# Split-product attention scores for the later query blocks, later selection rounds, and layer statistics with tokens on partitions

## What is computed

```
h = layer_norm(alpha * h + 0.5 * swiglu(h, ffn1...))          # first norm
h = layer_norm(alpha * h + hybrid_mixer(h, ...))              # second norm
h = layer_norm(alpha * h + 0.5 * swiglu(h, ffn2...))
...
# layer_norm
mu = mean(x); var = mean(square(x - mu)); (x - mu) * rsqrt(var + eps) * g + b
...
# attention, for each query block: top-k of the index scores, then
s = einsum('bqhc,bqkc->bqhk', q_lat, kv_sel) * ATT_HEAD_DIM ** -0.5
p = softmax(where(valid, s, -inf))
o = einsum('bqhk,bqkc->bqhc', p, kv_sel)
```

## Time and profile before

| what | us |
|---|---|
| median of 3 runs (lowest, highest) | 1013.48 (1012.99, 1014.37) |
| the profiled execution | 1013.6 |
| its span | 1011.9 |
| first FFN and first norm, until the first projection starts | 0 to 373.5 |
| projections, scan, selection | 373.5 to 530.3 |
| attention loop | 530.3 to 596.6 |
| output projection and second norm | 596.6 to 652.5 |
| second FFN and last norm | 652.5 to 1011.9 |

### The profile page before, as it was taken

One profiled execution on the slowest core, in us unless ns is written; L12 is line 12 of the kernel. 1 busy time (PEld: TensorE's weight loads), 2 busy tenths in 40 slices (PEclk: granted clock), 3 DMA queues, 4 the chain that ended last, 5 costly groups with the idle time before them and its releaser, 6 DMA issues.

```text
span 1011.9 us, 19045 instructions
## 1 busy us (share of the span) xinstructions
PE 992.6 (98%) x7048; PEld 911.2 (90%) x7048; DVE 718.1 (71%) x1299; ACT 500.2 (49%) x883; POOL 120.5 (12%) x96
## 2 busy tenths in 40 slices
PE   8999999999999999999999999999999999999996
PEld 8999999999999989699866778889999999988885
DVE  6988888888223263599998633699989989932336
ACT  6655655566221254546336732566656665812121
POOL 0000000000211253044221205310000000000000
PEclk9999999999999999999999999999999999999998
DMA  7223232323222323131210102113323233333212
GB/s 253 85 88 121 87 120 83 124 70 115 87 86 87 106 75 107 43 123 50 80 42 1 43 1 84 42 42 126 124 83 124 93 114 105 126 96 106 93 57 84
DMA packets 30847, 90.47 MB, mean 89 GB/s; under 512 B 4688, under 2 KB 5328, under 8 KB 30800
## 3 DMA queue, kind: packets, MB, share of 16 engines
q1 hardware_dynamic: 30800, 89.83, 27.0%
HBM read 87.72 MB, written 2.10 MB: 89 GB/s over the span
## 4 chain that ended last, share of the span: by engine, by line
PE 80%; DVE 15%; ACT 2%; issue 1%; DMA 1%; SPq 0%; DVEq 0%; ACTq 0%
PE ps L1253 38%; PE ps L1311 22%; PE ps L1176 9%; DVE sc L2244 3%; DVE top L2243 3%; PE ps L1448 1%; PE ps L1716 1%; PE ps L1730 1%; DVE qk L2283 1%; PE ps L1756 1%; DVE wlo L1920 1%; PE ps L1513 1%; PE ps L1361 1%; PE ps L1359 1%; DMA wraw<-in_ffn_w_up 1%
## 5 line engine op out<-in xcount | busy, mean ns | idle before, releaser
L1253 PE MATMUL ps<-tsum,whi 128*128 128x264 f32 (+1 forms) x1280 | 243.1, 282 | 0.5 <-ACT ht L813 0.5
L1253 PEld LDWEIGHTS ps<-tsum,whi 128*128 128x128 f32 x1280 | 202.3, 188 | 0.7 <-issue 0.7
L1253 PE MATMUL ps<-tsum,wlo 128*128 128x264 f32 (+1 forms) x640 | 180.3, 282 | 0.0
L1253 PE MATMUL ps<-xh,whi 128*128 128x264 f32 (+1 forms) x480 | 135.4, 282 | 0.3 <-ACT sil L813 0.3
L1253 PE MATMUL ps<-xl,whi 128*128 128x264 f32 (+1 forms) x480 | 135.5, 282 | 0.0
L752 ACT ACTIVATE whi<-wraw 128x1408 fp32r<-128x1408 f32 (+1 forms) x48 | 74.7, 1556 | 122.9 <-PE ps L1311 121.8
L1253 PE MATMUL ps<-xh,wlo 128*128 128x264 f32 (+1 forms) x480 | 135.3, 282 | 0.0
L1830 DVE TENSOR_TENSOR wlo<-wraw,whi 128x1408 fp32r<-128x1408 f32 (+1 forms) x38 | 70.1, 1845 | 85.9 <-ACT whi L752 85.9
L1311 PE MATMUL ps<-hh,whi 128*128 128x264 f32 (+1 forms) x462 | 124.2, 323 | 0.0
L1311 PE MATMUL ps<-hh,wlo 128*128 128x264 f32 (+1 forms) x462 | 123.5, 322 | 0.0
L1311 PE MATMUL ps<-hl,whi 128*128 128x264 f32 (+1 forms) x462 | 123.3, 321 | 0.0
(11 more groups left out here) (304 smaller groups left out, 1854.2 us busy)
## 6 DMA issues: line engine op xcount, KB each, us to landing
wraw<-in_ffn_w_gate SPq DMA_DIRECT2D x43, 512.0 KB, 4.2
wraw<-in_ffn_w_up SPq DMA_DIRECT2D x42, 512.0 KB, 4.4
wraw<-in_ffn_w_down SPq DMA_DIRECT2D x32, 384.0 KB, 3.2
wraw<-in_ffn_w_down SPq DMA_DIRECT2D x32, 320.0 KB, 3.5
wraw<-in_w_in SPq DMA_DIRECT2D x19, 512.0 KB, 4.4
wraw<-in_w_out SPq DMA_DIRECT2D x8, 512.0 KB, 4.4
out<-zrow SPq DMA_DIRECT2D x8, 256.0 KB, 2.0
x<-in_x SPq DMA_DIRECT2D x3, 528.0 KB, 7.5
```

The costliest lines, as they stand in the source:

```text
L1253: mm = pe.matmul(ps[:, bank, 0:(HT, HALF_SEQ)[p // 2]], w[:, k * P:(k + 1) * P], v[:, k, :], start=(first and k == 0 and n == 0), stop=(k ...
```

## The change

It has three parts, in one diff.

1. **Split-product scores.** For j of 3 and 4 (k of 16 and up) a score product is three f32r products: high part of the queries by high part of the keys, low part of the queries by high part of the keys, high part of the queries by low part of the keys. POOL makes all parts: `split_keys_hi` before `split_latents`, and behind it `split_queries` (two casts and two subtractions, each 128x4x256, waiting for the third head of `normed_mlstm`) and `split_keys_lo` (a subtraction, 128x528). PE waits for the six of them (`att_split`) at k=16. The high parts of the queries lie in `xh` and `xl`, which are free then.
2. **Selection rounds.** `LATE_AT` becomes (3, 4, 5).
3. **Layer statistics with tokens on partitions.** The sum tiles are now the stationary operand and one column of `mean_w` moves. p=0: 12 fp32 products of 88 token columns by one column for each half; p=1: 8 of 128. The statistics are then [88, 3] or [128, 2] wide on ACT and DVE. `spread_stat` brings mean and inverse deviation back to all partitions: 3 (p=0) or 2 (p=1) fp32 products with the identity, 88 or 128 columns wide, for each of both halves and both values. For p=0, e=0 they stand inside the down product, after kk=10 and kk=17. DVE's first scales of a half wait for the spread.

```diff
-LATE_AT = (2, 3, 4)
+LATE_AT = (3, 4, 5)
...
+SPLIT_J = 3
...
+    ql_low = sb("ql_low", [P, ATT_H, T], F32R, s)
...
+def query_hi(h):
+    return (xh if h < 4 else xl)[:, h % 4, :]
...
+def stat_tiles(p, e):
+    R = (HT // 3, P)[p]
+    t0 = e * HT if p == 0 else N_META + e * HALF_SEQ
+    return [(i, R, slice(t0 + i * R, t0 + (i + 1) * R)) for i in range(3 - p)]
+def token_sums(p, e, v):
+    return ps[0:(HT // 3, P)[p], 4 + 2 * v + e, 320:320 + 3 - p]
+def token_stat(p, e, v):
+    return stat[0:(HT // 3, P)[p], e, 4 * v:4 * v + 3 - p]
...
+        def split_keys_hi():
+            pool.wait_ge(ct_ready, 1)
+            pool.tensor_copy(ct_hi[:, :], ct[:, :]).then_inc(att_split, 1)
+        def split_keys_lo():
+            pool.wait_ge(att_split, 1)
+            pool.wait_ge(ql_done, ATT_H)
+            pool.tensor_tensor(ct_lo[:, :], ct[:, :], ct_hi[:, :].bitcast(F32), ALU.subtract).then_inc(att_split, 1)
+        def split_queries():
+            pool.wait_ge(ql_own, QL_DVE)
+            pool.wait_ge(ql_ready, ATT_H - QL_DVE)
+            pool.wait_ge(hn_ready, 3)
+            for e, v in enumerate((xh, xl)):
+                pool.tensor_copy(v[:, 0:4, LATE_T], ql[:, 4 * e:4 * e + 4, LATE_T]).then_inc(att_split, 1)
+            for e, v in enumerate((xh, xl)):
+                q = ql[:, 4 * e:4 * e + 4, LATE_T]
+                pool.wait_ge(att_split, e + 2)
+                pool.tensor_tensor(ql_low[:, 4 * e:4 * e + 4, LATE_T], q, v[:, 0:4, LATE_T].bitcast(F32), ALU.subtract).then_inc(att_split, 1)
         mix_lo(N_PROJ)
+        split_keys_hi()
         split_latents()
+        split_queries()
+        split_keys_lo()
...
-            act.activation(part(sil[:, 0, :], p, e), part_bank(4, p, e), ACT.Square).then_inc(s["mu2_done"], 1)
+            act.activation(token_stat(p, e, 0), token_sums(p, e, 0), ACT.Copy).then_inc(s["mu2_done"], 1)
+            act.activation(token_stat(p, e, 1), token_sums(p, e, 0), ACT.Square).then_inc(s["mu2_done"], 1)
             act.wait_ge(s["varc_done"], e + 1)
-            act.activation(part(sil[:, 1, :], p, e), part_bank(6, p, e), ACT.Sqrt).then_inc(s["sd_done"], 1)
+            act.activation(token_stat(p, e, 3), token_stat(p, e, 2), ACT.Sqrt).then_inc(s["sd_done"], 1)
...
                 if (e, kk) == (1, 7):
                     stats(0, 0)
+                if (e, kk) == (1, 10):
+                    spread_stat(0, 0, 0)
+                if (e, kk) == (1, 17):
+                    spread_stat(0, 0, 1)
...
-        for b, v in ((4, zsum), (6, ssum)):
-            pe.matmul(part_bank(b, p, e), mean_w[:, :], part(v, p, e), start=True, stop=False)
-            done, last = ("z_done", x[:, KT - 1, :]) if b == 4 else ("sq_done", sil[:, 1, :])
+        for v, (w, done, last) in enumerate(((zsum, "z_done", x[:, KT - 1, :]), (ssum, "sq_done", sil[:, 1, :]))):
             pe.wait_ge(s[done], KT + e)
-            pe.matmul(part_bank(b, p, e), mean_w[:, :], part(last, p, e), start=False, stop=True)\
-                .then_inc(s["stats_done"], 1)
+            for i, R, tokens in stat_tiles(p, e):
+                dst = token_sums(p, e, v)[:, i:i + 1]
+                pe.matmul(dst, w[:, tokens], mean_w[:, 0:1], start=True, stop=False)
+                mm = pe.matmul(dst, last[:, tokens], mean_w[:, 0:1], start=False, stop=True)
+            mm.then_inc(s["stats_done"], 1)
+    def spread_stat(p, e, v):
+        if v == 0:
+            pe.wait_ge(F[p]["mu2_done"], 2 * e + 2)
+        else:
+            pe.wait_ge(F[p]["rstd_done"], e + 1)
+        for i, R, _ in stat_tiles(p, e):
+            mm = pe.matmul(ps[:, 4 + 2 * v + e, i * R:(i + 1) * R],
+                           token_stat(p, e, 2 * v)[:, i:i + 1].broadcast_to([R, P]), ident[0:R, 0:R],
+                           start=True, stop=True)
+        mm.then_inc(stat_spread, 1)
+    def finish_stats(p):
+        if p == 1:
+            spread_stat(p, 0, 0)
+        stats(p, 1)
+        if p == 1:
+            spread_stat(p, 0, 1)
+        keep_warm(3)
+        spread_stat(p, 1, 0)
+        keep_warm(5)
+        spread_stat(p, 1, 1)
+        keep_warm(WARM_NORM - 12)
...
+            if j >= SPLIT_J:
+                if k % ATT_H == 0 and j == SPLIT_J:
+                    pe.wait_ge(att_split, 6)
+                q_h, q_l = query_hi(h)[:, START[j]:END[j]], ql_low[:, h, START[j]:END[j]]
+                for e in range(parts):
+                    dst = ps[:, 4 + 2 * (k % 2) + e, 0:w]
+                    pe.matmul(dst, q_h, ct_hi[:, e * w:(e + 1) * w], start=True, stop=False)
+                    pe.matmul(dst, q_l, ct_hi[:, e * w:(e + 1) * w], start=False, stop=False)
+                    mm = pe.matmul(dst, q_h, ct_lo[:, e * w:(e + 1) * w], start=False, stop=True)
+                mm.then_inc(s_done, 1)
+                return
...
-    stats(0, 1)
-    keep_warm(WARM_NORM)
+    finish_stats(0)
     mixer()
-    stats(1, 1)
-    keep_warm(WARM_NORM)
+    finish_stats(1)
...
         def variance(e):
-            var = part_bank(6, p, e)
+            var = token_stat(p, e, 2)
             dve.wait_ge(s["stats_done"], 2 * e + 2)
-            dve.wait_ge(s["mu2_done"], e + 1)
-            dve.tensor_tensor(var, var, part(sil[:, 0, :], p, e), ALU.subtract).then_inc(s["var_done"], 1)
+            dve.wait_ge(s["mu2_done"], 2 * e + 2)
+            dve.tensor_tensor(var, token_sums(p, e, 1), token_stat(p, e, 1), ALU.subtract).then_inc(s["var_done"], 1)
...
-            dve.reciprocal(part_bank(6, p, e), part(sil[:, 1, :], p, e)).then_inc(s["rstd_done"], 1)
+            dve.reciprocal(token_stat(p, e, 2), token_stat(p, e, 3)).then_inc(s["rstd_done"], 1)
...
         def half_centres(e, ks):
+            dve.wait_ge(stat_spread, 4 * p + 2 * e + 1)
...
         def half_scales(e):
-            dve.wait_ge(s["rstd_done"], e + 1)
+            dve.wait_ge(stat_spread, 4 * p + 2 * e + 2)
...
-        early = 3 if p == 0 else 1
+        early = 3 if p == 0 else 2
         last_residual(0)
-        variance(0)
-        half_centres(0, range(early))
         if p == 1:
             last_residual(1)
+        variance(0)
         inverse(0)
-        half_scales(0)
+        half_centres(0, range(early))
         if p == 0:
+            half_scales(0)
             last_residual(1)
         variance(1)
-        half_centres(1, range(min(early, 2)))
         inverse(1)
-        half_centres(1, range(2, early))
+        if p == 1:
+            half_scales(0)
+        half_centres(1, range(early))
         half_scales(1)
```

More of the change, by code:

```diff
@@ L127, in build @@
         vec = sb("vec", [P, NV])
+        stat = sb("stat", [P, 2, 16])
         zsum, ssum = ht[:, 0, :], ht[:, 1, :]
@@ L178, in build @@
             qa = sb("qa", [P, 4, T], F32, s)
-            ql = sb("ql", [P, ATT_H, T], F32, s)
+            with ExitStack() as ql_scope:
+                ql = sb("ql", [P, ATT_H, T], F32, ql_scope)
+            ql_low = sb("ql_low", [P, ATT_H, T], F32R, s)
             ct = sb("ct", [P, T], F32, s)
@@ L184, in build @@
             clo, chi = c_parts[:, :, 0:LAT], c_parts[:, :, LAT:2 * LAT]
-            wuk = sb("wuk", [P, 4, LAT], F32, s)
+            ct_hi = sb("ct_hi", [P, T], F32R, s)
+            with ExitStack() as wuk_scope:
+                ct_lo = sb("ct_lo", [P, T], F32R, wuk_scope)
+            with ExitStack() as wuk_scope:
+                wuk = sb("wuk", [P, 4, LAT], F32, wuk_scope)
+            sb("ct_lo_room", [P, T], F32, s)
             wuv = sb("wuv", [P, ATT_H, ATT_D], F32, s)
@@ L195, in build @@
             rows = sb("rows", [P, 2, T], F32, s)
-            kvg = sb("kvg", [P, LAT], F32, s)
+            with ExitStack() as kvg_scope:
+                kvg = sb("kvg", [P, LAT], F32, kvg_scope)
+            bst = sb("bst", [P, ML_H * 4, 6], F32, s)
+            mv = sb("mv", [P, ML_H * 4, 2], F32, s)
             bg = sb("bg", [P, 8], F32, s)
@@ L208, in build @@
             rinv = sb("rinv", [P, NT, ATT_H], F32, s)
-            bst = sb("bst", [P, ML_H * 4, 6], F32, s)
-            mv = sb("mv", [P, ML_H * 4, 2], F32, s)
             mls = sb("mls", [P, 3, ML_H * 4], F32, s)
@@ L300, in yml @@
             return (ht if h < 2 else rows)[:, h % 2, N_META:T]
+        LATE_T = slice(START[SPLIT_J], END[NT - 1])
+        def query_hi(h):
+            return (xh if h < 4 else xl)[:, h % 4, :]
         def turned_head(h):
@@ L343, in build @@
         half_done = sem("half_done")
+        stat_spread = sem("stat_spread")
         proj_evac = sem("proj_evac")
@@ L359, in build @@
         c_ready = sem("c_ready")
+        att_split = sem("att_split")
         ct_turned = sem("ct_turned")
```

## The result

The changed kernel takes 1015.36 us in the median of nine executions (1013.62 to 1016.58), the kernel before 1013.15 beside it (nine, 1012.50 to 1014.37). The ratio is 1.0019 (95% interval 1.0011 to 1.0028), so it is 2.2 us slower by the medians, about the 2.0 us that the prediction took as the limit of what can be told. The profiled execution took 1013.75 us, 1.6 less than the median; the nine differ by 3 us, and the longer ones have the lower mean granted clock (0.998 at 1013.62, 0.993 at 1016.58). The profiled execution is one of the three, and that must be kept in mind for every row of it.

The account below looks back on a forecast made before the run. PE was taken to bound most of the kernel (80% of the chain), with DVE or ACT counting where PE waits. Terms -2.5 + 1.3 - 0.4 = -1.6 took 1013.6 to 1012.0, 1011.9 us against the median; range 1009.9 to 1015.3.

Parts of the forecast that it names:

- Attention, -2.5: Attention: scores and rounds together -2.65, POOL's effect on DVE +0.15; -2.5 us, range -3.4 to -0.2.
- scores of block 3: PE, groups 4 and 5: eight heads each 0.18 us shorter; half counted since the chain is partly DVE's, -0.7.
- Block 4: PE, groups 6 and 7: eight heads each 0.18 us shorter where nobody is waited for, -1.4.
- The rounds: DVE's selection rounds: -0.5 us in group 2, -0.35 in group 4, +0.3 in group 5.
- The casts: POOL's casts of 1024 columns for the queries' parts: taken as 1.2 us each, bounds 0.3 and 2.3.
- rival 2: Attention: slow POOL casts hold DVE through the fourth head's norm, +2.3 us; 1014, no change; chance 0.15.
- First norm, +1.3: First norm: +1.6 us inside the down product and -0.3 in the tail, +1.3.
- In-line: First norm, inside the down product: short sums and two spreads on busy PE, +1.6 us (+1.3 to +2.5).
- The short product: First norm sums: an instruction of one moving and 88 weight columns taken as 0.08 us, bounds 0.074 and 0.108.
- The tail's -0.3: End of first norm: `xh` starts earlier, PE follows ACT from the second tile; -0.3 us (-0.6 to +0.6).
- rival 1b: First norm's sums inside the down product: one moving column loses the clock, +4 us, 1016; shared chance 0.15.
- Second norm, -0.4: Second norm: 0 in-line, two wide inverses go in the tail, second `xh` earlier; -0.4 us (-0.6 to +0.3).

Follow-up runs that it names:

- scores_only: Kernel before with the split scores alone, selection rounds and statistics as before; executed once, attention 64.91 us against 66.25 before.
- no_second: Changed kernel with the old statistics in the second norm; 1015.61 us, ratio 1.0021 to the kernel before.
- fill_wait: Changed kernel with three more dummy products ahead of the first norm's sums of half 1, where PE waits; 1013.88 us, ratio 1.0016.
- stats_only: Kernel before with the new layer statistics alone, in both norms, old scores and rounds; 1019.80 us, ratio 1.0055.
- sums64: Changed kernel with 64 moving columns in place of one in all products of the layer sums; 1013.76 us, ratio 1.0008.
- narrow_tail: Changed kernel with 64 moving columns in the sums, but one in the first norm's sums of half 1; 1015.40 us, ratio 1.0027.
- wide_dummies: Changed kernel with dummies of 512 moving columns (1, 1 and 2) for 3, 5 and 8 of 128, both norms; 1018.56 us, ratio 1.0056.
- second_end: Kernel before with split scores, later rounds, new statistics in second norm only (64 moving columns), `stat` behind all other tiles; 1011.03 us, ratio 0.9983.
- room128: Kernel before with an unused tile of 128 bytes per partition ahead of `xh`, `xl` and the FFN's tiles; 1014.24 us, ratio 1.0011.
- narrow_inner: Changed kernel with 64 moving columns in the sums, but one in the first norm's sums of half 0; 1013.67 us, ratio 1.0009.

## Why the prediction was wrong

The forecast was 1011.9 us and its range ended at 1015.3; 1015.36 was measured. Two steps failed. The granted clock was taken as 1.00 throughout, and its fall costs 1.6 us. The code that the diff leaves alone was taken as unchanged, and the second FFN grew by 1.2. The attention gave 0.6 less than forecast, the first norm cost 0.3 more, the second gave 0.15 less, and the kernel before was 0.3 below its older median: together the 3.5 us between forecast and result.

**Attention, -2.5: right in kind, -1.9 in size.** The mis-sized term is the scores of block 3: half of 1.4 was counted, and 0.13 came, because each is 0.11 rather than 0.18 shorter and because PE then waits for DVE there (0.41 and 0.18 us in scores_only). Block 4 gave 1.22 for 1.4. The rounds gave 0.61 for 0.55, and that this sum fits is luck: ahead of k=16 they gave 0.90 where 0.5 was said to be all that can go, and in groups 4 and 5 they cost 0.26 where the sum of the two terms was -0.05. The casts took 1.04 each for 1.2, POOL's last part ended at 543.5, and PE did not wait. POOL held DVE as rival 2 said, for 0.9 us, at no cost. The Trainium skill, "GPSIMD Engine Reference", Key points, names DVE ops in a 2-port mode or with two SBUF inputs; here a TENSOR_SCALAR with one tile as input was held (2.00 for 1.11), and no row tells in which mode it ran.

**First norm, +1.3: +1.58 undisturbed, and wrong in the median.** In-line came 1.5 for 1.6 (from the sums of half 0 to those of half 1, without the wait: 366.05 - 359.18 = 6.87 before; the last down product ends its issue at 367.03, 8.38 behind 358.65). The short product is 0.078 where 0.08 was taken. The Trainium skill, "TensorE: Matmul & The Clock Gate", LDWEIGHTS, gives 73 ns for 88 columns; the row is 5 ns over it. The tail's -0.3 did not come: the first product is +0.07, and the second tile's, where the gain was expected, only -0.03 (374.89 - 359.18 = 15.71 before, 375.84 - 358.65 = 17.19, against 1.51 in-line). The dummies start 0.53 later behind the down product, not 0.4, and the first `xh` 3.84 behind them, not 3.75. What failed is the step that took the granted clock as 1.00 and put the fall, rival 1b, into a shared chance of 0.15. It was placed at the sums inside the down product with a price of 4 us; it came behind those of the tail, with a price of 1.6 in the traces of no_second and fill_wait and of 3.25 in that of stats_only, and by times and mean clocks in six of nine executions of the changed kernel. That rival 1b's 1016 lies near the median is luck in size: its +4 stood for a fall elsewhere, and the 1.2 of the second FFN was in no rival. Its mechanism, products of one moving column that lose the clock, was the right one: sums64 removes the loss and narrow_tail brings it back. The Trainium skill, "TensorE: Matmul & The Clock Gate", Part 1, says that the granted clock follows the array's activity. The runs with the sums agree (one moving column against 64); wide_dummies, with as many moved columns behind the sums and the clock lost for longer, is not explained by it.

**Second norm, -0.4: -0.25.** DVE now idles ahead of its scales until the second spread. Its timeline, and TensorE's first products, beside the earlier trace rows:

```profile
650.40 0.75 DVE L2245 TENSOR_TENSOR x<-x,ps 128x256 f32<-128x256 f32 x2 [0.81 <-PE ps L1500]
```

```profile
651.90 0.48 PE L1232 MATMUL ps<-xh,whi 128*128 128x512 f32 x1
...
653.13 0.50 PE L1232 MATMUL ps<-xh,whi 128*128 128x512 f32 x1
```

Counted from the first output product, PE's first product comes 0.22 later (55.97 to 56.19), the one that waits for ACT's second part 0.25 earlier (654.23 - 596.56 = 57.67 before, 653.13 - 595.71 = 57.42): -0.25, too little to be seen in second_end.

**What was in no step: +1.2.** All the sums took the code that the diff leaves alone as unchanged, a term put at nothing without a reason. The diff adds a tile of 128 bytes ahead of others, and the second FFN grows by 1.2 us (room128). The line was in the diff; no price stood on it.

The account closes: in us, +1.6 first norm, -1.9 attention, -0.25 second norm, +1.2 place of the tiles, +1.6 for the clock is +2.2, and the medians differ by 1015.36 - 1013.15 = 2.2. The last term is the 1.6 between the median and the undisturbed execution, and the fall in no_second's trace has the same size.

## What to carry to other kernels

Before a product is made narrow because its weights set its rate, look what the clock stands on there: 64 moving columns cost as much time as one (15.95 and 15.94 us for the stage) and kept the clock in all eleven executions of sums64. A profiled execution can miss what the median holds, so compare its time and its mean clock with those of the other executions before a row is believed. A new tile belongs behind the others, or its shift has to be tried by itself with the old code.

## What the runs showed of the hardware

- Short fp32 products are issued 0.078 us an instruction with 88 weight columns, with 1 or with 64 moving columns alike (changed kernel and sums64), and 0.11 with 128 (646.32 to 646.54 in the changed kernel, two instructions).
- In the tail of the first norm the granted clock fell to 1.2 GHz behind 24 instructions of one moving column (traces of no_second and stats_only), also where no wait stood ahead of them (fill_wait). By the mean clocks that happened in most executions and not in all: six of nine of the changed kernel, eight of nine of narrow_tail. Inside a stream of 264-column products the same 24 left it at 2.4 GHz in the trace of narrow_inner, and its eleven executions lie within 0.9 us.
- Moving the FFN's tiles by 128 bytes per partition slows TensorE's stream of 256-column products in the second FFN by 0.7% (424 products for 427 in 50 us), moving them by 256 does not (427). The 264-column stream of the first FFN is not slowed (823 and 822 in 100 us).
- A POOL cast of 128x1024 takes 1.04 us, less than half of the subtraction of that size (2.37), both in the changed kernel.
